# Three attentions pipelined by one more tile, index weights as an eight-row unit, modulation columns in two chains and none in the projections

## The reference, cut to what matters

```
mod = silu(c) @ ada_w + ada_b                        # six vectors of 1024: 48 columns of 128
u = rmsnorm(x) * (1 + scale1) + shift1
aq, ak, av, bq, bkv, biq, bik, biw, cq, ck, cv, g = split(u @ w_in)
y_a = diff_attention(aq, ak, av) @ w_br_a            # softmax rows p0 - lam * p1, 4 heads
score = sum_h relu(biq_h . bik) * biw_h              # 8 index heads, weights biw
sel = top_k(score, 128)
y_b = dsa_attention(bq, rmsnorm(bkv), sel) @ w_br_b  # 4 heads over the selected keys
y_c = moba_attention(cq, ck, cv) @ w_br_c            # 4 heads, causal blocks
x = x + gate1 * (sum_n sigmoid(g_n) * y_n) @ w_o
u2 = rmsnorm(x) * (1 + scale2) + shift2              # then the MLP, with gate2
```

## Time and profile before

| | |
|---|---|
| runs | 3103.05 us median of 3 (3100.77 to 3106.71) |
| profiled execution | 3100.33 us |
| its span, first to last instruction | 3098.6 us |
| TensorE busy | 2726.4 us (88%) |
| VectorE busy | 1570.9 us (51%) |
| ScalarE busy | 1071.9 us (35%) |
| GpSimd busy | 481.7 us (16%) |
| granted TensorE clock, mean | 0.927 |
| HBM traffic | 80 GB/s over the span |

### The profile page before, as it was taken

The page is one execution under the profiler, slowest core; times in us unless marked ns, Lnnn a source line. Parts: engine busy times, 40 slices in busy tenths (PEclk is TensorE's granted clock), DMA queues, the critical chain, the costliest instruction groups (busy, mean ns, idle before and its releaser), DMA issues.

```text
span 3098.6 us, 29866 instructions
## 1 busy us (share of the span) xinstructions
PE 2726.4 (88%) x11893; PEld 2140.9 (69%) x11893; DVE 1570.9 (51%) x2443; ACT 1071.9 (35%) x1690; POOL 481.7 (16%) x342
## 2 busy tenths in 40 slices
PE   6878696888999989977779989999799899899996
PEld 4656364666888877766667668888568687578885
DVE  3565657535433237956676464332563563543333
ACT  2223343333433222432444343322442353343322
POOL 1021131321000014432311020000101210200001
PEclk7887797999999989989889999999899999899998
DMA  7442211223333322300223123333121142133331
GB/s 205 110 118 68 75 55 29 83 66 91 89 95 95 95 75 82 96 21 21 89 83 96 54 69 96 95 95 96 48 75 55 48 127 64 55 89 95 96 95 54
DMA packets 481274, 251.07 MB, mean 81 GB/s; under 512 B 13534, under 2 KB 478002, under 8 KB 481135
## 3 DMA queue, kind: packets, MB, share of 16 engines
q1 hardware_dynamic: 478516, 242.43, 27.3%
q0 software_dynamic: 1904, 5.73, 0.6%
q10 hardware_dynamic: 715, 1.01, 0.1%
HBM read 247.00 MB, written 2.13 MB: 80 GB/s over the span
## 4 chain that ended last, share of the span: by engine, by line
PE 73%; DVE 16%; ACT 6%; DMA 2%; issue 2%; POOL 1%; SPq 0%; DVEq 0%; ACTq 0%; POOLq 0%
PE ps L741 20%; PE ps L743 20%; PE ps L739 20%; DVE adat L2001 2%; DVE ps L1890 2%; DMA w_f<-in_w_in 2%; PE ps L905 1%; PE ps L1142 1%; PE ps L821 1%; ACT arena_f L1483 1%; DVE hT L2474 1%; ACT wh L1273 1%; DVE w_r L1858 1%; PE ps L890 1%; PE ps L1121 1%
## 5 line engine op out<-in xcount | busy, mean ns | idle before, releaser
L739 PE MATMUL ps<-XH,wh 128*128 128x512 f32 x2160 | 878.8, 407 | 51.0 <-ACT XH L1727 26.5
L743 PE MATMUL ps<-XH,w_r 128*128 128x512 f32 x2160 | 866.3, 401 | 9.9 <-DVE w_r L1858 9.2
L741 PE MATMUL ps<-XL,wh 128*128 128x512 f32 x1968 | 796.2, 405 | 3.9 <-DVE XL L1863 3.9
L1858 DVE TENSOR_TENSOR w_r<-w_f,wh 128x1024 fp32r<-128x1024 f32 x328 | 400.5, 1224 | 556.3 <-ACT wh L1273 556.0
L1273 ACT ACTIVATE wh<-w_f 128x1024 fp32r<-128x1024 f32 (+2 forms) x423 | 429.0, 1017 | 445.3 <-PE ps L743 365.0
L739 PEld LDWEIGHTS ps<-XH,wh 128*128 128x128 f32 x2160 | 418.1, 194 | 172.8 <-ACT XH L1727 30.2
L743 PEld LDWEIGHTS ps<-XH,w_r 128*128 128x128 f32 x2160 | 415.5, 192 | 110.0 <-DVE w_r L1858 12.6
L741 PE MATMUL ps<-arena_r,wh 128*128 128x512 f32 (+1 forms) x1280 | 481.4, 376 | 0.0
L741 PEld LDWEIGHTS ps<-XL,wh 128*128 128x128 f32 x1968 | 380.0, 193 | 96.0 <-DVE XL L1863 7.3
L743 PE MATMUL ps<-arena_r,w_r 128*128 128x512 f32 (+1 forms) x944 | 347.3, 368 | 10.9 <-DVE w_r L1858 8.5
L739 PE MATMUL ps<-arena_r,wh 128*128 128x512 f32 (+1 forms) x944 | 354.5, 375 | 1.4 <-ACT wh L1273 1.4
(11 more groups left out here) (308 smaller groups left out, 2757.4 us busy)
## 6 DMA issues: line engine op xcount, KB each, us to landing
w_f<-in_mlp_w SPq DMA_DIRECT2D x128, 512.0 KB, 3.9
w_f<-in_w_ff SPq DMA_DIRECT2D x64, 512.0 KB, 3.8
w_f<-in_w_in SPq DMA_DIRECT2D x49, 512.0 KB, 3.7
w_f<-in_ada_w SPq DMA_DIRECT2D x48, 512.0 KB, 4.6
w_f<-in_even_w_in SPq DMA_DIRECT2D x36, 512.0 KB, 3.6
w_f<-in_odd_w_in SPq DMA_DIRECT2D x24, 512.0 KB, 3.7
w_f<-in_xa_w_v SPq DMA_DIRECT2D x16, 512.0 KB, 3.5
w_f<-in_even_w_out SPq DMA_DIRECT2D x16, 512.0 KB, 3.6
```

The lines of the kernel that those rows point to most:

```text
L739: e.matmul(b, hi[:, k, :], xh, start=u.first and k == 0, stop=False)
L741: e.matmul(b, hi[:, k, :], xl, start=False, stop=False)
L743: last = e.matmul(b, lo[:, k, :], xh, start=False, stop=u.final and k == u.kc - 1)
L1858: e.tensor_tensor(flat(u, 1), flat(u, 0), high_flat(u).bitcast(F32), ALU.subtract).then_inc(dve.sem, dve.up("low", u.n))
```

## The change

Five things. (1) In the three attentions the finish of a tile moves one step later: VectorE finishes the rows of tile i-1 at the head of step i (diff) or does a top-k round between maximum and reciprocal (moba); the product with the values, its norm and its low parts come one or more steps after the transposes. (2) The units are spread anew: none in most steps that begin a head, cq and ck in the index stage, all steps of moba used. (3) The index weights (8 columns), 96 small matmuls before, become an ordinary product with eight output rows, transposed afterwards. (4) `ada_sum` runs two chains, even and odd chunks, and TensorE adds the two; none in the projections, one in each of the six index steps, and the last eight columns (40 to 47) as eight one-column products each on TensorE, three in branch b and five after the sum of r0. (5) The sigmoid's scale and offset move from GpSimd into VectorE's product and a factor of one half afterwards; the weights of `wuv` are loaded before the attentions.

```diff
+ADA_LATE = 40
-    rest = iter(ada[16:])
+    rest = iter(ada[16:ADA_LATE])
-    plans["project"] = project[:3]
-    for u in project[3:]:
-        plans["project"] += [u, next(rest)]
+    plans["project"] = project
...
     for i in range(17):
-        plans["diff", i] = [u for u in (next(fill, None), next(rest)) if u]
+        plans["diff", i] = [next(fill)] if i % 4 and i < 15 else []
+        plans["diff", i] += [next(rest)] if i % 4 < 2 else []
...
+        return gates[:1] + [u for two in zip(gates[1:], outs) for u in two] + outs[-1:]
-    fill = iter(branch(0, A["w_br_a"][0], "ya"))
+    fill = iter(columns_of("cq", w_in, COL_CQ, 256, "X0") + columns_of("ck", w_in, COL_CK, 256, "X0")
+                + branch(0, A["w_br_a"][0], "ya"))
     for i in range(6):
-        plans["index", i] = [next(fill)]
+        plans["index", i] = [next(fill), next(rest)]
     for i in range(17):
-        plans["moba", i] = [u for u in (next(fill, None),) if u]
+        plans["moba", i] = [u for u in (next(fill, None) if i % 4 or i in (8, 12) else None,) if u]
...
+        plans["dsa", i] = [next(fill)] if i else []
+        plans["dsa", i] += [next(rest)] if i % 4 < 2 else []
+    plans["b first"], plans["b second"], plans["b fill"] = units[:1], units[1:2], ada[ADA_LATE:ADA_LATE + 3]
+    plans["branch b"] = units[2:]
     plans["w_o"] = columns_of("wo", A["w_o"][0], 0, D, "X1", lead=True)
+    plans["r0 fill"] = ada[ADA_LATE + 3:]
...
# tensor_program
-            for i, (h, qt) in enumerate(tiles):
-                if i % NT == 1 and i > NT:
-                    rms_sums(("a", h - 1), 1)
...
+            for i in range(17):
+                if i < 16:
+                    h, qt = tiles[i]
+                    for m in range(2):
+                        rows = slice(DH * m, DH * (m + 1))
+                        scores(("a", h, qt, m), aq[rows, h, qt * P:(qt + 1) * P], ak[rows, h, 0:(qt + 1) * P], qt,
+                               (act, "aq", h), (act, "ak", h))
+                run(("diff", i))
+                if i % 4 == 1 and i >= 5:
+                    diff_out((i - 5) // 4)
+                if i:
+                    h, qt = tiles[i - 1]
+                    turn_rows(("a", h, qt), ws_diff, ("a", h, qt, 0), qt, dve)
+                if i % 4 == 2 and i >= 6:
+                    rms_sums(("a", (i - 6) // 4), 1)
...
             rms_sums("r0", KC)
+            ada_late("r0 fill")
             run((0, "ff1"))
...
# scalar_program
             rms("r0", D, 0, stat[:, 0, :])
             modulated(1, "X2")
+            run("r0 fill")
...
# vector_program
-                e.tensor_scalar(a, wt[:, 0, :], cond[:, 0, :], None, ALU.mult).then_inc(dve.sem, dve.up())
-                for k in range(1, KC):
-                    w.wait_ge(dve, dve.count)
-                    e.scalar_tensor_tensor(out=a, in0=wt[:, k, :], scalar=cond[:, k, :], in1=a, op0=ALU.mult, op1=ALU.add).then_inc(
-                        dve.sem, dve.up("ada sum", u.m))
+                for k in range(2):
+                    e.tensor_scalar(a[:, k, :], wt[:, k, :], cond[:, k, :], None, ALU.mult).then_inc(dve.sem, dve.up())
+                for k in range(2, KC):
+                    w.wait_ge(dve, dve.count - 1)
+                    e.scalar_tensor_tensor(out=a[:, k % 2, :], in0=wt[:, k, :], scalar=cond[:, k, :], in1=a[:, k % 2, :],
+                                           op0=ALU.mult, op1=ALU.add).then_inc(dve.sem, dve.up("ada sum", u.m))
...
+            for i in range(17):
                 if i:
                     diff_end(*tiles[i - 1])
+                if i < 16:
+                    h, qt = tiles[i]
+                    for m in range(2):
+                        rows_begin(ws_diff, ("a", h, qt, m), qt, DH ** -0.5, h)
...
+                    rows_begin(ws_rows, ("c", h, qt), qt, DH ** -0.5, 8 + h)
+                    top_round(2, 3)
+                    rows_sum(("c", h, qt))
```

More of the change, by code:

```diff
@@ L256, in plan @@
     fill = iter(branch(2, A["w_br_c"][0], "yc"))
-    rest = iter([*rest, Step("ada end")])
     for i in range(17):
-        plans["dsa", i] = [u for u in (next(fill, None), next(rest, None)) if u]
-    plans["branch b"] = branch(1, A["w_br_b"][0], "yb")
+        plans["dsa", i] = [next(fill)] if i else []
+        plans["dsa", i] += [next(rest)] if i % 4 < 2 else []
+    assert not next(rest, None) and not next(fill, None)
+    units = branch(1, A["w_br_b"][0], "yb")
+    plans["b first"], plans["b second"], plans["b fill"] = units[:1], units[1:2], ada[ADA_LATE:ADA_LATE + 3]
@@ L506, in program @@
         iw, o = area(o, NT, 8)
-        top8, o = area(o, 8)
+        tops, o = area(o, NT - 1, 8)
+        adat, o = area(o, 4, P)
+        ada_ring = Ring("ada", [adat[:, 2 * j:2 * j + 2, :] for j in range(2)], rings)
         pick = stat
@@ L987, in tensor_program, with latent_out, latent_values @@
-            run(("dsa", 16))
-            latent_end(*tiles[-1])
-            for g in range(2):
+                    h, qt = tiles[i - 1]
+                    turn_rows(("c", h, qt), ws_rows, ("c", h, qt), qt, act)
+            def latent_out(h):
+                b, freed = att_out.take("o", "b", h)
+                w.wait_ge(*freed)
+                w.wait_ge(act, "kv")
+                weigh(("b", h), b, lambda kt: kv[:, kt, :], True, True)
+            def latent_values(g):
                 b, freed = lin.take("wuv", g)
@@ L998, in tensor_program @@
                     pe.sem, pe.up("wuv", g))
+            for i in range(17):
+                if i < 16:
+                    h, qt = tiles[i]
+                    scores(("b", h, qt), bq[:, h, qt * P:(qt + 1) * P], kvT[:, 0:(qt + 1) * P], qt,
+                           (act, "bq", 3), (dve, "kvT"))
+                run(("dsa", i))
+                if i == 0:
+                    block_out(HEADS - 1)
+                if i % 4 == 1 and i >= 5:
+                    latent_out((i - 5) // 4)
+                if i:
+                    h, qt = tiles[i - 1]
+                    turn_rows(("b", h, qt), ws_rows, ("b", h, qt), qt, act)
+                if i == 11:
+                    latent_values(0)
+            run("b first")
+            latent_out(HEADS - 1)
+            ada_total(ADA_LATE - 1)
+            run("b second")
+            latent_values(1)
+            ada_late("b fill")
             run("branch b")
@@ L1560, in scalar_program @@
-            run(("dsa", 16))
-            rows_turned(("b", 3, 3), 3, "o", "b", 2)
-            for g in range(2):
-                high_part(bias_r[:, 4 + g, :], lin.of("wuv", g)[:, :], "yb", g, (pe, "wuv", g))
+                    h, qt = tiles[i - 1]
+                    rows_turned(("b", h, qt), qt, "o", *(("b", h - 1) if h else ("c", 3)))
+                if i == 11:
+                    high_of_values(0)
+            run("b first")
+            run("b second")
+            high_of_values(1)
@@ L2008, in ada_total, with ada_late @@
                 att_now[0].free(dve, "ada", m)
+            def ada_late(stage):
+                us = plans[stage]
+                m, n = us[0].m, len(us)
+                for u in us:
+                    lower_ahead(u.n)
+                w.wait_ge(pe, "unit", us[-1].n)
+                e.tensor_tensor(modc[:, m:m + n], att_now[0].of(stage)[:, m:m + n], columns("ada_b", m, n), ALU.add).then_inc(
+                    dve.sem, dve.up("late mod", stage))
+                att_now[0].free(dve, stage)
             def memory_part(li, k):
@@ L2252, in vector_program, with low_of_values @@
+            def low_of_values(g):
                 low_part(ob_r[:, g, :], lin.of("wuv", g)[:, :], bias_r[:, 4 + g, :], "yb", g)
                 lin.free(dve, "wuv", g)
+            for i in range(17):
+                if i < 16:
+                    h, qt = tiles[i]
+                    rows_begin(ws_rows, ("b", h, qt), qt, P ** -0.5, 4 + h, pick[:, qt - 1, 0:(qt + 1) * P] if qt else None)
+                    if i == 1:
+                        low_of_pair(1)
+                    if i % 4 == 2 and i >= 6:
+                        latent_out((i - 6) // 4)
+                    if i == 12:
+                        low_of_values(0)
+                    rows_sum(("b", h, qt))
+                run(("dsa", i))
@@ L2254, in vector_program @@
+            run("b first")
+            latent_out(HEADS - 1)
+            ada_total(ADA_LATE - 1)
+            run("b second")
+            low_of_values(1)
+            ada_late("b fill")
             run("branch b")
```

462 lines of the change are left out of this document (224 added, 238 removed).

## The result

| | before | after |
|---|---|---|
| median | 3101.91 us (3098.99 to 3106.71) | 2987.84 us (2982.05 to 2991.80) |
| ratio | 1 | 0.9631 [0.9613, 0.9649] |
| profiled execution | 3100.33 us | 2989.61 us |
| its span | 3098.6 us | 2987.9 us |
| mean granted clock | 0.927 | 0.939 |

Foretold were 2969 us in a range of 2930 to 3012. The gain is 114 us where the sum gave 134.

The account below looks back on a forecast made before the run. The bound was taken to be TensorE's order of work and its waits for chains of small steps. Stage terms summed to -134.2 us, taking the profiled execution from 3100.33 to 2966; median 2969 us, range 2930 to 3012.

Parts of the forecast that it names:

- project, diff, index: First three stages: project 91.6 to 71.4 us, diff 212.6 to 105, index 43.9 to 60.
- -20.2 and -12.3: Project stage without columns gains 20.2 us; in diff the index weights fall from 18 us of TensorE to 5.7.
- VectorE gets six sums, 16 rounds and a norm: 56 us: Index stage: this work on top of its weighting makes VectorE the bound, so the stage takes 60 us.
- 8.5 for this, for the end and for the clock together: Moba: 8.5 us for the start's wait, the end and two clock falls, on 81.5 of TensorE, giving 90.
- VectorE above 0.9 in the index stage: Sign that the forecast is right: VectorE's busy share there above 0.9, with TensorE waiting for it.
- 4 for stalls in dsa: Dsa, branch b and w_o: 4 us of stalls allowed in dsa, within a gain of 16.9 us.
- the loss foretold: R0: ff1's first rounding falls behind the eighth chunk, its first pair is done after 32.5 us; loss 12.2.
- 1.1+5x2.2: R0: TensorE's time for the five late columns, given as 11 us, after which it idles.
- (a): Rival: VectorE becomes the bound in diff too, diff 120 and moba 100 us, about 3004 in all; chance 0.18.
- (b): Rival: stalls left in are hidden, no waits at the ends, ff1 starts as before, 2931 us; chance 0.13.
- (c): Rival: slower, short waits keep TensorE at 1.2 GHz through the attentions, 3125 us at 60% low level; chance 0.04.
- (d): Rival: interleaved chains gain nothing, or loads set diff's pace, the latter 3048 us; chance 0.05.

Follow-up runs that it names:

- e5: The kernel before, with only the project stage's modulation columns taken out, so that the third attention has fifteen instead of six: 3106.40 us, ratio 1.0012.
- e6: The kernel before, with only the index weights made an ordinary unit with eight output rows instead of 96 small matmuls: 3099.37 us, ratio 0.9990.
- e3: The kernel after, with the five late columns moved from behind r0 into branch b as VectorE sums: 2970.84 us, ratio 0.9577.
- e8: The kernel after, with the third attention's nine columns in every second step instead of in pairs: 2986.49 us, ratio 0.9618.
- e12: The kernel after, with VectorE's order of before in the first two attentions and TensorE's order kept: 2986.09 us, ratio 0.9629.
- e11: The kernel after, with nine columns back in the project stage and none in the third attention: 2999.93 us, ratio 0.9673.
- e9: The kernel after, unchanged, run once more: 2987.97 us, ratio 0.9632.
- e1: The kernel after, with each modulation sum as one dependent chain of seven plus one alone instead of two interleaved chains: 3000.79 us, ratio 0.9666.
- e10: The kernel after, with the index weights as 96 matmuls of eight columns again: 2998.10 us, ratio 0.9664; its profiled execution is not used.

## Why the prediction was right, and where its 19 us went

**Right: project, diff, index.** 71 for 71.4, 105 for 105, 60 for 60, which is 112 us, where the profiled executions lie 110.7 us apart in all. The mechanisms of the first two are what the profile now shows: TensorE busy for all of project, for 98 of 105 us in diff, at a granted clock of 0.97 and 0.98 (0.90 and 0.79 in the earlier trace rows). Diff's end is bare as foretold, three waits of 1.9, 2.4 and 0.5 us. Of diff's 107 us, 46 are TensorE's idle time (52.9 before, 6.8 now) and 61 its busy time. By the prediction's prices 23 of the 61 are the four units that left and 12 the index weights; the rest I put mainly to the clock, which is an estimate. Index has the right number by luck, as is told below.

**But not part by part.** These stage times were worked out for the whole new schedule, and that is why they held. Read as prices of single parts they are wrong: e5 and e6 alone moved the time by +3.8 and -3.3 us, where their terms read -20.2 and -12.3. Before, TensorE, VectorE and ScalarE took turns at the path, and time freed on one went into a wait for another. Only with all parts is TensorE the bound of project and diff, and then undoing one costs 10 us for the index weights (12.3 priced), 12 for the project columns, 13 for the chains and 11 for the lag of the product. These four sum to some 47 of 114 us. The rest is the spread of the units, the sigmoid, the early load for `wuv` and what the parts do for each other, which no run takes apart: that the spread brings it is argued, not shown.

**Index and moba's start: the step "VectorE gets six sums, 16 rounds and a norm: 56 us", mis-sized.** The work came to 49 us, 40 in the stage and 9 behind it, and it was added up as if VectorE could begin at once. It waited for 12.2 us for totals that TensorE issues behind its unit, and its first rows of moba came 69.5 us after the stage's start. Index came out at 60 by luck: VectorE did not set its length. TensorE was busy for 54.9 of 60 us, where 49 were foretold at full clock (granted 0.87), and waited for 4.9. Then it went on into moba and met the backlog there: 9.3 us, where I had 8.5 for this, for the end and for the clock together. "VectorE above 0.9 in the index stage" was wrong too (0.67; 31 of 37 us, 0.84, from 289 on). This is 9 us, part of it run-to-run (moba ends 3 us sooner in e3, e8 and e12).

**Dsa: the step "4 for stalls in dsa", mis-sized.** e11 against e9 prices nine columns there at 9.4 us; three waits for sums in neighbouring steps are 4.0 of it (5.2 in the trace of after). e8 takes them away. Besides, the first 6.6 us of dsa in after ran at 0.50. The values' part was right in size: the wait for `wuv` of 5.2 us is gone, and the three columns took 6.65 us from 536.91. That is 2.2 each only because 3.9 us of it fell on the full level and 2.7 on the low one. Branch b and w_o took 3 us more than foretold. The 2.5 us of waits at w_o, counted as gone, are still there and now 3.3 (2.7 for the low part of the input and 0.6 for its high part, 1.4 and 1.0 before), and the clock was 0.94 over these 121 us, where 2.6 us were allowed for it. How the 3 us divide is not shown.

**R0: the loss foretold, by two steps of which one was wrong.** 12.2 us foretold, 11.7 in the trace of after and 15 in e9's. The order of ScalarE was the right reason: its rounding came 17.5 us after w_o (17.1 foretold). The columns' price of 2.2 us was not: the earlier trace rows shows a column that began at the low level and ended at the full one, and behind r0 all five ran at the low one, 3.4 us each, 17.1 us instead of 11. So TensorE is free only when the weights are there (660.3 us for the first low part, 660.9 for the pair). Two limits fell together, and the error cost little. What I did not ask is whether the columns had to stand there: as VectorE sums they cost some 4 us (e3). The prediction's 1.1+5x2.2 is 12.1 and not 11; nothing hangs on it, since the weights come later.

**The chains.** 2.05 us a sum against 2.1 foretold, from one start gap in the earlier trace rows. Their worth was put at 6 us, e1 gives 10 up to r0 in its trace and 13 in the median: I had counted the sum as on the path in two places, and it is on it in diff and dsa as well.

**The first stage: sign wrong.** One us less was foretold, 3.4 more is in the trace; nine traces of kernels with two chains have it at 84.0 to 89.8, mean 87.6, three with the old sum at 85.2 to 86.5. In after the load of the first project unit is issued at 68.1 us instead of 62.7, and the granted clock from 40 us to its end is 0.57 instead of 0.65. Whether the two totals per column, the clock or the loads begin it is not settled; no run isolates it.

**The sum of the misses.** The profiled execution was foretold at 2966 us and took 2989.6. By stages the 23.6 us are 9 in moba, 8 in dsa, 3 in branch b and w_o and 4.4 in the first stage, less 0.5 each in project and r0. The medians lie 19 us apart, because the median of after is 1.8 below its profiled execution and was foretold 2.7 above it.

**Rivals.** (a) did not come: VectorE was busy for 83 of 105 us in diff, less than the 92 foretold, and TensorE for 98. (b) did not either: diff's end, moba's start and r0 all had the waits that it takes away. (c) did not, though the clock did not rise everywhere: it went from 0.90 to 0.97 in project, 0.79 to 0.98 in diff, 0.83 to 0.91 in moba and 0.91 to 0.96 in dsa, and fell from 0.91 to 0.87 in index, from 1.00 to 0.94 in branch b and w_o and from 0.83 to 0.69 behind r0. (d)'s part on the chains is refuted by e1, and TensorE waited for no load in diff.

## What to carry to other kernels

Price a reordering by stages of the new schedule as a whole: where engines take turns on the path, a single part may bring nothing alone (e5, e6) and its full length in company (e10, e11). Before adding up an engine's work in a stage, ask which of its instructions wait for another engine's late ones, and lay the rest end to end behind them; a backlog surfaces in the next stage. Small work put into a gap has to be asked what it delays behind it and at which clock it runs: the five columns in the gap behind r0 cost 13.5 to 17.6 us, and some 4 us as VectorE sums beside full units. A price read from one row holds for the clock of that row.

## What the runs showed of the hardware that I had not expected

Products of one column keep TensorE busy without a gap for 17 us and the granted clock stays at 0.50; a column then takes 3.4 us instead of 1.8 at the full level. In branch b the clock fell to 0.50 while such products ran, after full-size work at 1.00 and without a gap (from 540.8 us in after, 536.5 in e9). The 96 matmuls of eight columns in before have the same start gaps, 0.11 us at the full level and 0.21 at the low one, and the clock fell during them too (at 293.0 us, from 290.6 to 309). On VectorE an instruction of 128 elements that waits for its predecessor's result starts 0.39 us behind it, one that waits for the result before that 0.26. While GpSimd forms low parts the first ones are longer; the groups of after in diff (161 to 266 us), where the records alone last 0.34 and 0.28 us:

```profile
L2043 DVE SCALAR_TENSOR_TENSOR arena_f<-w_f,modc,arena_f 128x128 f32<-128x128 f32 x54 | 17.0, 382 | 0.0
...
L2040 DVE TENSOR_SCALAR arena_f<-w_f,modc 128x128 f32<-128x128 f32 x18 | 8.7, 620 | 0.0
```

The first instruction of a sum took 1.02 us in the mean in the earlier trace rows and takes 0.62 here. The mean hides two kinds: of seventeen in before ten took 0.28 us with no GpSimd instruction beside them, and six that began under a low part took 2.30 to 2.40 us and ended within 0.1 us of it. In after three sums began under a low part; their first instruction took 0.58 to 2.30 us and the second 0.27 or 0.28. So of two in a row the wait for GpSimd was paid once. In a fourth sum, beside GpSimd filling a tile with zeros, both ran side by side for 1.8 to 2.0 us.
